# First mixer's preparation: gating bias in one product per group, value products by tile, query rotations between them, and its small loads issued a stage earlier

## The reference, cut to what matters

```python
u, v, q, c_kv, q_idx, k_idx, w_idx, gates = jnp.split(proj, SPLIT_OFFSETS, axis=-1)
# spatial gating, 4 groups of 128 features, chunks of 128 tokens
u = jax.nn.gelu(u)
v = layer_norm(jax.nn.gelu(v), v_g, v_b)
w = jnp.where(causal[None], w_s, jnp.zeros_like(w_s))
z = jnp.einsum('gts,bcsgd->bctgd', w, v) + b_s.T[None, None, :, :, None]
y_a = u * z
# attention operands
c_n = rms_norm(c_kv, kv_norm_g[l])
k = rms_norm(c_n @ w_uk[l], k_norm_g[l])
vv = c_n @ w_uv[l]
qh = rms_norm(q.reshape(bsz, s, N_HEADS, HEAD_DIM), q_norm_g[l])
qh, k, qi, ki = partial_rope(...) of each, with cos and sin of position times frequency
wi = w_idx * (IDX_HEADS ** -0.5)
```

## Time and profile before

| | us |
|---|---|
| median of 3 runs | 3141.58 |
| the profiled execution | 3127.38 |
| its span | 3125.6 |
| TensorE busy in the span | 2970.7 (95%) |
| VectorE busy | 1776.4 (57%) |
| ScalarE busy | 1037.8 (33%) |
| GpSimd busy | 794.3 (25%) |

### The profile page before, as it was taken

How to read it: one execution, slowest core, us unless ns; L and a number is a source line. 1 busy time by engine, 2 the same in 40 slices (tenths; PEclk the granted TensorE clock), 3 DMA queues, 4 the chain that set the end, 5 groups by cost and what they waited for, 6 DMA issues and landing times. The chain is left out here.

```text
span 3125.6 us, 40997 instructions
## 1 busy us (share of the span) xinstructions
PE 2970.7 (95%) x14434; PEld 2519.8 (81%) x14434; DVE 1776.4 (57%) x3714; ACT 1037.8 (33%) x1471; POOL 794.3 (25%) x493
## 2 busy tenths in 40 slices
PE   8779889999999999989999999999999999899996
PEld 6657767888888888879999998888877776688885
DVE  6554444956767774038888886443263555364423
ACT  4222332333344444223333333322132235242221
POOL 0023200544433333457666640000010320000000
PEclk9879999999999999999999999999999998999998
DMA  4013322344444455479999992333241100133331
GB/s 148 19 60 109 108 106 90 125 135 143 143 146 168 171 187 195 142 239 383 360 356 350 354 349 84 95 95 101 88 164 68 34 28 1 66 104 97 99 94 61
DMA packets 175037, 458.34 MB, mean 147 GB/s; under 512 B 21425, under 2 KB 71217, under 8 KB 172722
## 3 DMA queue, kind: packets, MB, share of 16 engines
q1 hardware_dynamic: 151074, 363.97, 34.8%
q0 software_dynamic: 22528, 67.19, 5.7%
q10 hardware_dynamic: 1296, 25.36, 1.9%
HBM read 391.25 MB, written 65.01 MB: 146 GB/s over the span
## 5 line engine op out<-in xcount | busy, mean ns | idle before, releaser
L54 PE MATMUL cb_y<-cb_g_hi,ex_hi 128*128 128x384 f32 x1024 | 343.9, 336 | 10.2 <-DVE cb_g_lo L1796 10.2
L55 PE MATMUL cb_y<-cb_g_lo,ex_hi 128*128 128x384 f32 x1024 | 343.5, 335 | 0.0
L56 PE MATMUL cb_y<-cb_g_hi,ex_lo 128*128 128x384 f32 x1024 | 343.5, 335 | 0.0
L425 POOL TENSOR_TENSOR ex_lo<-ex_raw,ex_hi 128x1024 fp32r<-128x1024 f32 x96 | 243.8, 2541 | 349.1 <-ACT ex_hi L411 349.0
L195 DVE TENSOR_TENSOR ffn_lo<-ffn_raw,ffn_hi 128x1024 fp32r<-128x1024 f32 x130 | 159.2, 1226 | 260.2 <-ACT ffn_hi L191 260.1
L54 PE MATMUL ffn_bank<-x_hi,ffn_hi 128*128 128x512 f32 x704 | 275.9, 392 | 12.0 <-DVE x_lo L250 10.9
L56 PE MATMUL ffn_bank<-x_hi,ffn_lo 128*128 128x512 f32 x704 | 278.7, 396 | 0.0
L55 PE MATMUL ffn_bank<-x_lo,ffn_hi 128*128 128x512 f32 x704 | 277.5, 394 | 0.0
L54 PE MATMUL bs_ps<-x_hi,ex_hi 128*128 128x512 f32 x576 | 232.3, 403 | 3.8 <-PEq L44 3.8
L56 PE MATMUL bs_ps<-x_hi,ex_lo 128*128 128x512 f32 x576 | 226.8, 394 | 0.0
L55 PE MATMUL bs_ps<-x_lo,ex_hi 128*128 128x512 f32 x576 | 225.1, 391 | 0.0
(11 more groups left out here) (506 smaller groups left out, 6477.8 us busy)
## 6 DMA issues: line engine op xcount, KB each, us to landing
ex_raw<-in_peer_u SPq DMA_DIRECT2D x96, 512.0 KB, 3.5
ex_raw<-in_peer_v SPq DMA_DIRECT2D x96, 512.0 KB, 8.2
ffn_raw<-in_gu SPq DMA_DIRECT2D x86, 512.0 KB, 3.5
hidden<-up_out SPq DMA_DIRECT2D x128, 256.0 KB, 2.2
routing<-br_out ACTq DMA_DIRECT2D x8, 3072.0 KB, 9.0
cb_route<-routing SPq DMA_DIRECT2D x32, 768.0 KB, 9.2
cb_unit<-hidden SPq DMA_DIRECT2D x128, 192.0 KB, 6.8
ffn_raw<-in_down SPq DMA_DIRECT2D x44, 512.0 KB, 3.5
```

What stands on the lines that cost most here:

```text
L54: pe.matmul(out, w_high, x_high, start=first, stop=False)
L55: pe.matmul(out, w_high, x_low, start=False, stop=False)
L56: return pe.matmul(out, w_low, x_high, start=False, stop=last)
L425: eng.tensor_tensor(self.lo[:, s, :], self.raw[s], self.hi[:, s, :].bitcast(F32), ALU.subtract).then_inc(self.split, 1)
```

## The change

The small tiles get a class of their own, made before the projection, and their loads are handed to the projection stage as `then_load`. On TensorE the bias of a group is one product over all four token tiles, first into its bank; the value products go tile by tile, each waiting for its own value tile; the turns of the queries stand between and behind them and write banks 0 to 3 under a semaphore of their own (`q_turned`), so they are no jobs any more. VectorE rotates q0 and q1 ahead of the gatings and q2 and q3 behind the key's norm, and makes the cosines ahead of `sum_q`.

```diff
+class Smalls:
+    def __init__(self, c):
+        self.wsT = c.sb("m1_wsT", [P, A_GROUPS, P])
...
+        self.count = 16 * 8
+    def load(self, sp, d):
+        sp.dma_start(self.posi[:], d["positions"].rearrange("a s -> (a s)").partition_broadcast(P)
+                     ).then_inc(self.positions, 16)
+        sp.dma_start(self.inv[:], d["inv"]).then_inc(self.positions, 16)
+        sp.dma_start(self.rot[:], d["rot"]).then_inc(self.landed, 16)
...
-                 "rstd_q3", "sum_k"] + [f"z{g}" for g in range(A_GROUPS)] + ["rstd_k"]
-                + [f"rot_q{h}" for h in range(N_HEADS)] + ["rot_k", "wi"])
+                 "rstd_q3", "sum_k"] + [f"z{g}" for g in range(A_GROUPS)] + ["rstd_k", "rot_k", "wi"])
...
                 mean_square("sum_c", SUMS_OF["c"], TILES, KV_LATENT)
-                mean_square("sum_q", SUMS_OF["q0"], TILES * N_HEADS, P)
                 for kind in (R128, R64):
                     dve.wait_ge(S["sines"], 2 * kind + 2)
                     then(dve.tensor_tensor(cos[kind][:], cos[kind][:], cos[kind][:], ALU.mult))
                     then(dve.tensor_scalar(cos[kind][:], cos[kind][:], -2.0, 1.0, ALU.mult, ALU.add))
+                mean_square("sum_q", SUMS_OF["q0"], TILES * N_HEADS, P)
...
+                def rope_query(h):
+                    tile = proj[:, Q0 + h, :]
+                    dve.wait_ge(S["q_turned"], h + 1)
+                    then(dve.tensor_tensor(tile, tile, cos[R128][:], ALU.mult))
+                    then(dve.tensor_tensor(turned[:], banks[h][:], sin[R128][:], ALU.mult))
+                    then(dve.tensor_tensor(tile, tile, turned[:], ALU.add))
+                rope_query(0)
+                rope_query(1)
                 for g in range(A_GROUPS):
                     take(f"z{g}")
...
                 normed("k", kT[:], gains[:, 3:4])
-                for i, x in enumerate(QK):
-                    rope(f"rot_{x}", kT[:] if x == "k" else proj[:, Q0 + i, :], R128)
+                rope_query(2)
+                rope_query(3)
+                rope("rot_k", kT[:], R128)
...
                 pe.wait_ge(S["masked"], 1)
-                pe.wait_ge(S["vnorm"], TILES)
                 for g in range(A_GROUPS):
                     start(f"z{g}")
-                    for t in range(TILES):
-                        out = bank(f"z{g}")[:, t * P:(t + 1) * P]
-                        pe.matmul(out, vn[:, t, g * P:(g + 1) * P], wsT[:, g, :], start=True, stop=False)
-                        last = pe.matmul(out, ones[0:1, :], bs[:, g, :], start=False, stop=True)
-                    finish(last)
+                    pe.matmul(bank(f"z{g}")[:], ones[0:1, :], bs[:, g, :].unsqueeze(1).broadcast_to([1, TILES, P]),
+                              start=True, stop=False, skip_group_check=True)
+                pe.wait_ge(S["normed"], 1 + N_HEADS)
+                for t in range(TILES):
+                    pe.wait_ge(S["vnorm"], t + 1)
+                    for g in range(A_GROUPS):
+                        last = pe.matmul(bank(f"z{g}")[:, t * P:(t + 1) * P], vn[:, t, g * P:(g + 1) * P], wsT[:, g, :],
+                                         start=False, stop=t == TILES - 1, skip_group_check=True)
+                        if t == TILES - 1:
+                            finish(last)
+                    if t:
+                        pe.matmul(banks[t - 1][:], rot[:, R128, :], proj[:, Q0 + t - 1, :], start=True, stop=True
+                                  ).then_inc(S["q_turned"], 1)
+                pe.matmul(banks[TILES - 1][:], rot[:, R128, :], proj[:, Q0 + TILES - 1, :], start=True, stop=True
+                          ).then_inc(S["q_turned"], 1)
                 pe.wait_ge(S["rstd"], 2)
                 spread("k")
-                pe.wait_ge(S["normed"], 1 + N_HEADS)
-                for h in range(N_HEADS):
-                    turn(f"rot_q{h}", R128, proj[:, Q0 + h, :])
...
+            with ExitStack() as preparing:
+                smalls = Smalls(Chip(nc, preparing))
+                norm_and_project(nc, first, "p1", hT, x_hi, x_lo, gains.of("norm1_g"), d["w_in1"], proj, plain,
+                                 lambda sp: smalls.load(sp, d), x_landed=x_landed)
+                gate_and_prepare(nc, smalls, proj, kT, vv, wi, ident, ya_hi, ya_lo)
```

More of the change, by code:

```diff
@@ L776, with gate_and_prepare @@
 N_PROJ1 = 18
-def gate_and_prepare(nc, proj, kT, vv, wi, ident, ya_hi, ya_lo, d):
+class Smalls:
+    def __init__(self, c):
+        self.wsT = c.sb("m1_wsT", [P, A_GROUPS, P])
+        self.bs = c.sb("m1_bs", [1, A_GROUPS, P])
+        self.vg = c.sb("m1_vg", [P, SEQ])
+        self.vb = c.sb("m1_vb", [P, SEQ])
+        self.gains = c.sb("m1_gains", [P, 4])
+        self.wuk = c.sb("m1_wuk", [P, 2, P])
+        self.wuv = c.sb("m1_wuv", [P, 2, P])
+        self.rot = c.sb("m1_rot", [P, 2, P])
+        self.inv = c.sb("m1_inv", [P, 2])
+        self.posi = c.sb("m1_posi", [P, SEQ], I32)
+        self.landed, self.positions = c.sem("m1_small"), c.sem("m1_positions")
+        self.count = 16 * 8
[4 more added lines that the diff above has]
+        sp.dma_start(self.rot[:], d["rot"]).then_inc(self.landed, 16)
+        sp.dma_start(self.gains[:], d["gains"]).then_inc(self.landed, 16)
+        sp.dma_start(self.wuk[:], d["wuk"]).then_inc(self.landed, 16)
+        sp.dma_start(self.wuv[:], d["wuv"]).then_inc(self.landed, 16)
+        sp.dma_start(self.wsT[:], d["wsT"]).then_inc(self.landed, 16)
+        sp.dma_start(self.bs[:], d["bs"]).then_inc(self.landed, 16)
+        sp.dma_start(self.vg[:], d["vg"].partition_broadcast(P)).then_inc(self.landed, 16)
+        sp.dma_start(self.vb[:], d["vb"].partition_broadcast(P)).then_inc(self.landed, 16)
+def gate_and_prepare(nc, smalls, proj, kT, vv, wi, ident, ya_hi, ya_lo):
     with ExitStack() as ctx:
@@ L785, in gate_and_prepare @@
         ones = c.sb("m1_ones", [P, P])
[L786 to L795, removed]
+        wsT, bs, vg, vb, gains = smalls.wsT, smalls.bs, smalls.vg, smalls.vb, smalls.gains
+        wuk, wuv, rot, inv, posi = smalls.wuk, smalls.wuv, smalls.rot, smalls.inv, smalls.posi
         pos = c.sb("m1_pos", [P, SEQ])
@@ L812, in gate_and_prepare @@
         S = {x: c.sem(f"m1_{x}") for x in (
-            "small", "positions", "const", "masked", "gelu", "vt", "ln_var", "ln_sd", "vnorm", "seq",
+            "const", "masked", "q_turned", "gelu", "vt", "ln_var", "ln_sd", "vnorm", "seq",
             "sq", "job", "took", "ms", "root", "rstd", "half", "angle", "sines", "normed", "gated", "low")}
-        small, job, took, seq = S["small"], S["job"], S["took"], S["seq"]
-        SMALL = ["wsT", "bs", "vg", "vb", "gains", "wuk", "wuv", "rot"]
+        small, job, took, seq = smalls.landed, S["job"], S["took"], S["seq"]
         R128, R64 = 0, 1
         JOBS = (["sum_c", "sum_q", "rot_qi0", "rot_qi1", "rstd_c", "rot_ki", "rstd_q0", "rstd_q1", "k", "rstd_q2", "vv",
-                 "rstd_q3", "sum_k"] + [f"z{g}" for g in range(A_GROUPS)] + ["rstd_k"]
-                + [f"rot_q{h}" for h in range(N_HEADS)] + ["rot_k", "wi"])
+                 "rstd_q3", "sum_k"] + [f"z{g}" for g in range(A_GROUPS)] + ["rstd_k", "rot_k", "wi"])
         SUMS_OF = {"c": 0, **{f"q{h}": TILES * (1 + h) for h in range(N_HEADS)}, "k": TILES * (1 + N_HEADS)}
@@ L824, in gate_and_prepare @@
         SQS = ["c0", "c1"] + [f"q{h}" for h in range(N_HEADS)] + ["k"]
-        QK = [f"q{h}" for h in range(N_HEADS)] + ["k"]
         def bank(x):
@@ L830, in gate_and_prepare @@
         with nc.Block() as block:
[L831 to L843, removed]
             @block.gpsimd
@@ L851, in _ @@
                                    pattern=[[-1, P]], channel_multiplier=1).then_inc(S["const"], 1)
-                pool.wait_ge(small, 16 * len(SMALL))
+                pool.wait_ge(small, smalls.count)
                 pool.affine_select(out=wsT[:], in_=wsT[:], compare_op=ALU.is_ge, fill=0.0, base=0,
@@ L902, in _ @@
                 ROUND = 12582912.0
-                dve.wait_ge(S["positions"], 32)
+                dve.wait_ge(smalls.positions, 32)
                 then(dve.tensor_copy(pos[:], posi[:]))
@@ L950, in rope @@
                     then(dve.tensor_tensor(tile, tile, turned[:], ALU.add))
-                dve.wait_ge(small, 16 * len(SMALL))
+                dve.wait_ge(small, smalls.count)
                 mean_square("sum_c", SUMS_OF["c"], TILES, KV_LATENT)
-                mean_square("sum_q", SUMS_OF["q0"], TILES * N_HEADS, P)
                 for kind in (R128, R64):
@@ L1020, in _ @@
                     last.then_inc(S["vt"], 1)
-                pe.wait_ge(small, 16 * len(SMALL))
+                pe.wait_ge(small, smalls.count)
                 def sums(x, squares, at):
@@ L1093, in _ @@
                 finish(last)
-    clear_semaphores(nc, S.values())
+    clear_semaphores(nc, [*S.values(), smalls.landed, smalls.positions])
 def select_keys(nc, proj, wi, select, w_gates, x_hi, x_lo, gates):
@@ L1342, in first_mixer @@
                      for i in range(4)]
```

(2 more changed lines are left out.)

1 line of the change is left out of this document (removed).

## The result

Kernel after: median 3108.7 us of 4 runs (3106.06 to 3116.39); kernel before beside it: 3142.51 us (3140.47 to 3143.73). The direction was right, the size wrong.

The account below looks back on a forecast made before the run. The first mixer's preparation was taken as bound by VectorE, then TensorE, then VectorE, uncovered. Tail 20.8 plus head 2.6, less 0.1 for a semaphore, saved 23.3 us: 3141.58 to 3118.3 us, range 3113 to 3126.

Parts of the forecast that it names:

- the saving is the same there: Last step: the profiled execution's 23.3 us saving carried to the median of runs, 14.2 us above it.
- the stages behind start as before: Stages after the first mixer's preparation start from a full stop and a TensorE that had idled, as before.
- The tail: Preparation after the normalized values: VectorE runs unbroken, 15.35 us for 37.64; 20.8 us saved after 1.5 for GpSimd.
- GpSimd's port: Low parts of ya delay q2's rotation: first product about 1.0 us, sum about 0.5, so 1.5 us added.
- The bias products: First mixer's preparation, TensorE: one row by 512 columns each, 1.02 us at the high clock, bounds 0.95 and 2.9.
- The broadcast operand: Rival: the bias product's row read through a step of zero is slow; kernel slower from 7.4 us each; chance 0.03.
- The head: Preparation's start: earlier loads and cosines start VectorE's unbroken run 2.6 us sooner, range 0.5 to 3.6.
- the first index rotation: Sign of being right: VectorE's first index rotation in the preparation comes near 134.1 us.
- The small loads: Ten loads moved behind the projection's last panel split cost nothing; uncovered they would cost 1.6 us.
- The low clock: Rival: TensorE stays slow and bounds the preparation, 3124.6 us, or 3120.3 if the clock returns; wholly or partly 0.15.
- its rival: ScalarE's sines bind, so VectorE's run in the preparation starts only 0.5 us earlier, for 2.6: 3120.4 us; chance 0.11.
- the two that had no change or a loss: Products still wait for everything, 3141.6 us, chance 0.05; slow reading of the bias row makes the kernel slower, 0.03.

Follow-up runs that it names:

- experiment 1: The kernel before, unchanged, timed against itself and traced again: 3142.72 us, ratio 0.9998.
- experiment 2: The kernel after, unchanged, timed and traced again: 3108.44 us, ratio 0.9895 to the kernel before.
- experiment 4: 18 unread products added in TensorE's 4.6 us idle time in the second mixer: kernel before 3118.01 us, kernel after 3098.48 us.
- experiment 5: Unread products ahead of the sixth panel of the second mixer's attention: kernel before with one 3129.96 us, kernel after with 14 3124.43 us.
- the hold: 18 unread products added where TensorE idles in the second mixer's attention: kernel before 3118.01 us, kernel after 3098.48 us.
- the tail alone: Kernel before with only the new order of products, gatings and rotations: 3109.17 us; with the 18 unread products too, 3095.74 us.
- experiment 3: Kernel before with only the new order of products, gatings and rotations: 3109.17 us; with only the early loads and cosines: 3142.62 us.
- experiment 8: 18 unread products added: kernel after with an unused 384-byte tile too, 3095.45 us; kernel before with only the new product, gating and rotation order, 3095.74 us.
- experiment 6: Kernel after with an unused 384-byte tile that puts the projection's panels back at 320 bytes behind a multiple of 2048: 3105.0 us, ratio 0.9898.
- pad: Unused 384-byte tile between small tiles and projection's: kernel after 3105.0 us; with the 18 unread products too, 3095.45 us.
- head alone: Kernel before with only the early small loads and the cosines ahead of the query sums: 3142.62 us, ratio 0.9994.
- pairs by tile: Kernel after with the 16 pairs of value and bias product back, still tile by tile with turns between: 3137.93 us, ratio 0.9983.

## Why the prediction was wrong

**The step that failed** is the last of the sum: "the saving is the same there". The forecast carried the saving over from an execution at 3127.38 to a median 14.2 us above it, with the words "outside of anything the change touches". The distance was one stage's stretch at clock 0.50, 17.1 us long in the execution traced and 51.2 in the one of experiment 1; the change shifts that stage in time by some 18 to 24 us, and in the traces of after the stretch is 23.9 us long (experiments 1, 2, 4, 5). Of the 33.8 us, 14.3 are that; without them the change as made is worth 19.5, less than the 23.3 forecast. The sentence that "the stages behind start as before" is true of the engines and not of the clock. That 17.1 stood in the trace that the forecast was read from was a hint that was there to be seen: a granted clock of 0.52 for 17.5 us, behind an idle time of 4.6.

**Sizes, one by one.**
- The tail, forecast at 20.8: measured 37.64 - 16.17 = 21.5 where VectorE never waited, 19.8 in the execution with 1.52 us of waiting. With the hold the tail alone makes 3118.01 - 3095.74 = 22.3 us of the kernel. Right.
- Two rotations before the gatings, those 0.83 apart, the key's norm 0.9 behind: as written.
- GpSimd's port, forecast at 1.0 + 0.5: the first product of q2 took 1.47 (0.78 over 0.69), the sum 0.92 (0.23 over). 1.0 for 1.5. The rule of the Trainium skill named there, "SBUF — State Buffer", "Who interferes with whom", agrees: of q2's three rotation instructions only those with both operands in SBUF were delayed, beside the low parts of ya; L1004 with its PSUM operand kept its 0.69.
- The bias products, forecast at 1.02 and bounded by 0.95 and 2.9: 0.92 at the high clock, just under the bound, 1.43 where it was low for a part (5.71 / 4). The broadcast operand costs nothing that shows, so that rival falls.
- The head, forecast at 2.6: within the stage it is right, 2.9 us where the sums of squares ran at the same low clock (experiment 3). After's run starts 17.2 us into the stage, for 21.9, so 4.7 us; the other 1.8 are the clock, high for part of the sums (7.14 us for 10.40), as it also was in the unchanged kernel of experiment 1 (7.99). That the first index rotation came at 134.11, for a forecast of 134.1, is luck: the stage began 2.1 us later than forecast, and the clock gave 1.8 back. In the whole kernel the medians give the head 0.3 us with the hold (experiment 8), and do not settle it. The forecast ended its sum at the stage's last instruction; where the stages behind gave the rest back the two executions do not tell.
- The small loads: "they cost nothing" holds of the queue and not of the memory. Their tiles, and four more that went ahead of the projection with them, moved the panels: the projection lost 2.1 us in the traces (experiment 6), and the kernel 3.0 with the hold (experiment 8). The forecast had no term for it.

With hold and pad in place the change saves 3118.01 - 3095.45 = 22.6 us, for 23.3. That this is so near is in part luck: the tail brings 22.3 of it, 1.5 more than its 20.8, and the head 0.3 for 2.6. The mechanism of the tail was right; the carrying over to the median was not.

**The rivals.** The low clock came, in part: 0.63 over 3.7 us behind the bias products in one execution. The tail took 16.2 us in four traces (after, after with 14 products, after with the hold, and with hold and pad), 16.5 in two (after with the pad, tail alone with the hold) and 17.8 in two (after again, tail alone), so it cost between nothing and 1.6 us, for the forecast's 2 of a clock that comes back. The head gained 2.9 us in the stage, and not the 0.5 of its rival. No run supports the two that had no change or a loss.

**Open.** Why before and its relatives arrive at the long stretch and after at the one of 24 us. From the first of that stage's products without a reader, which every kernel here has (`hp_ps<-hp_hi`), to the clock's fall it is 10.30 to 10.34 us in the four traces with 51.2 us (before again, head alone, after with 14 products, pairs by tile), and 9.64 to 10.15 in the four with 23.9 (after, after again, tail alone, before with one product); but 10.45 and 10.04 (the first execution of before, after with the pad) gave 17.1. So the place of the work against the fall goes with the length in eight of ten traces and does not fix it alone; what rule makes the lengths is not shown. Nor is it why panels at 1984 bytes cost 5 ns a product: that their place does it is shown, and the mechanism is not. Nor what the head is worth in the whole kernel.

## What to carry to other kernels

When a trace lies more than a few tenths of a per cent from the median, find the stage that makes the distance before a saving is carried over: here it was worth 14.3 of 33.8 us, and one unread product more took 12.4 us off. Look in every stage for a low granted clock behind an idle time of TensorE, since filling 4.6 us with unread products brought 24.4 us; and hold that stage when a change elsewhere is to be measured. Keep the tiles of matmul operands at their addresses when tiles are added ahead of them, or compare the products' distance before and after.

## What the runs showed of the hardware

- The clock fell right behind four products of one row, with TensorE busy all the time before (1.00 over 3.70 of 3.70 us, then 0.63), and stayed at 0.50 through 23 us of products that alternate between 1 and 128 rows (in that trace the clock is low from 150.85 to 184.98) and through 49.8 busy us of 52 in the second mixer, though in another execution of the same kernel it rose after 17 us there.
- A product of 1 row by 512 columns took 0.92 us at the high clock, in a row of four (3.69 us); a turn of 128 rows by 512 columns took 1.02 by itself. One row is not cheaper in any proportion to its rows.
- Products of 512 columns in a projection came 227 ns apart with the panels at 320 bytes behind a multiple of 2048, and 232 ns at 1984.
- Switching ScalarE from exponential to silu to square root and back took three loads of 1.28 us.
